# Four weight casts of the first block, each written in two halves one attention unit apart

## The reference, cut to what matters

```python
hx = rms_norm(x, norm_pre[l]) * (1.0 + sc_x) + sh_x
px = hx @ w_in                 # 1024 x 4096
qa, ka, va, ga, bb, cb, ub, gb = jnp.split(px, 8, axis=-1)
s = jnp.einsum('bqhmd,bkhmd->bhmqk', q, k).astype(jnp.float32) * (A_QK ** -0.5)
p = jax.nn.softmax(s, axis=-1)
a = p[:, :, 0] - lam * p[:, :, 1]
o = jnp.einsum('bhqk,bkhd->bqhd', a, v.astype(jnp.float32))
```

## Time and profile before

| | us |
|---|---|
| median of 3 runs | 1646.39 |
| the three runs | 1647.64, 1646.39, 1641.05 |
| the profiled execution | 1641.94 |
| its span | 1640.2 |
| TensorE busy in the span | 1532.1 (93%) |
| ScalarE busy in the span | 665.6 (41%) |

### The profile page before, as it was taken

One profiled execution on the slowest core, in us unless ns is written; L12 is line 12 of the kernel. 1 busy time (PEld: TensorE's weight loads), 2 busy tenths in 40 slices (PEclk: granted clock), 3 DMA queues, 4 the chain that ended last, 5 costly groups with the idle time before them and its releaser, 6 DMA issues. The chain is left out here.

```text
span 1640.2 us, 29691 instructions
## 1 busy us (share of the span) xinstructions
PE 1532.1 (93%) x12509; PEld 1311.9 (80%) x12509; DVE 763.1 (47%) x1244; ACT 665.6 (41%) x1087; POOL 421.7 (26%) x107
## 2 busy tenths in 40 slices
PE   4899999999999999998989999977879999999998
PEld 3688898888887878987879897846768888888786
DVE  3544137777775510137854425468563333433002
ACT  2411216766653411127754444362354444344112
POOL 1422221111140243220022342200034333444342
PEclk9999999999999999999999999989999999999999
DMA  9244462244041032146220532000021222222321
GB/s 376 110 155 155 155 181 65 65 104 104 27 159 47 1 128 83 47 146 162 46 103 3 178 99 91 1 0 3 4 105 52 103 102 102 95 85 77 129 86 68
DMA packets 32598, 155.76 MB, mean 95 GB/s; under 512 B 6744, under 2 KB 8280, under 8 KB 18016
## 3 DMA queue, kind: packets, MB, share of 16 engines
q1 hardware_dynamic: 31168, 153.24, 28.3%
q10 hardware_dynamic: 1312, 0.80, 0.2%
HBM read 132.01 MB, written 2.10 MB: 82 GB/s over the span
## 5 line engine op out<-in xcount | busy, mean ns | idle before, releaser
L215 PE MATMUL banks<-ffn_token_parts,ffu_weight_parts 128*128 128x512 f32 (+1 forms) x1056 | 229.6, 380 | 1.2 <-POOL ffu_weight_parts L196 0.9
L215 PEld LDWEIGHTS banks<-ffn_token_parts,ffu_weight_parts 128*128 128x128 f32 x1056 | 191.7, 188 | 39.0 <-POOL ffu_weight_parts L196 1.1
L196 POOL TENSOR_TENSOR even_weight_parts<-weight_chunk,even_weight_parts 128x2048 fp32r<-128x2048 f32 x16 | 74.6, 4663 | 322.9 <-ACT even_weight_parts L190 322.9
L196 POOL TENSOR_TENSOR ffu_weight_parts<-weight_chunk,ffu_weight_parts 128x2048 fp32r<-128x2048 f32 x22 | 101.6, 4619 | 157.3 <-ACT ffu_weight_parts L190 157.3
L215 PE MATMUL banks<-even_token_parts,even_weight_parts 128*128 128x512 f32 x720 | 133.4, 345 | 0.0
L215 PEld LDWEIGHTS banks<-even_token_parts,even_weight_parts 128*128 128x128 f32 x720 | 110.8, 188 | 20.6 <-issue 3.8
L871 PE MATMUL banks<-even_token_parts,even_weight_parts 128*128 128x512 f32 (+1 forms) x576 | 122.3, 347 | 0.0
L3035 PE MATMUL banks<-ffd_weight_parts,ffn_f_parts 128*128 128x512 f32 x528 | 120.1, 389 | 1.6 <-PEq L2936 1.6
L3035 PEld LDWEIGHTS banks<-ffd_weight_parts,ffn_f_parts 128*128 128x128 f32 x528 | 99.0, 188 | 22.5 <-issue 2.0
L215 PE MATMUL banks<-sec_token_parts,sec_weight_parts 128*128 128x512 f32 (+1 forms) x528 | 114.1, 373 | 0.3 <-PEq L283 0.3
L3013 DVE SCALAR_TENSOR_TENSOR ffn_conv<-banks,b_ffn_taps,ffn_conv 128x511 f32<-128x511 f32 (+1 forms) x88 | 61.8, 744 | 111.9 <-ACT ffn_conv L2985 108.8
(11 more groups left out here) (449 smaller groups left out, 2808.5 us busy)
## 6 DMA issues: line engine op xcount, KB each, us to landing
weight_chunk<-in_ffn_up SPq DMA_DIRECT2D x22, 1024.0 KB, 4.8
weight_chunk<-in_w_in_even SPq DMA_DIRECT2D x16, 1024.0 KB, 6.9
front_late<-in_w_mod SPq DMA_DIRECT2D x16, 1024.0 KB, 4.9
weight_chunk<-in_w_in SPq DMA_DIRECT2D x13, 1024.0 KB, 4.8
weight_chunk<-in_w_out SPq DMA_DIRECT2D x12, 1024.0 KB, 5.4
weight_chunk<-in_w_in_odd SPq DMA_DIRECT2D x12, 1024.0 KB, 4.8
weight_chunk<-in_ffn_down SPq DMA_DIRECT2D x11, 1024.0 KB, 4.9
front_w<-in_w_mod SPq DMA_DIRECT2D x8, 1024.0 KB, 13.3
```

The source lines that it names most:

```text
L196: self.nc.gpsimd.tensor_tensor(parts[:, 1], self.env.raw[s][:], parts[:, 0].bitcast(F32), ALU.subtract).then_inc(self.lo_done, 1)
L215: m = self.nc.tensor.matmul(o, w, env.tok[:, tp, k, a:b], start=n == 0, stop=n == 3 * KD - 1)
```

## The change

The high parts of chunks 12 to 15 are no longer cast by one instruction after unit `c_after(n)`. The first four of the eight rows of k (1024 of 2048 columns a partition) are cast there, the other four after the next unit, `c_after(n) + 1`. Only the second half raises `hi_done`. Both wait for the same semaphores as the whole cast did. The second half stands ahead of the convolution copy (L1032) that follows the same unit for n = 21 and 23.

```diff
+    def hi_half(self, act, i, s, half, freed):
+
+        act.wait_ge(self.env.raw_in[s], self.base[s] + 16 + 16 * i)
+        act.wait_ge(*freed)
+        k = slice(half * KD // 2, (half + 1) * KD // 2)
+        m = self.nc.scalar.copy(self.slot(2 * i + s, s)[:, 0, k], self.env.raw[s][:, k])
+        if half:
+            m.then_inc(self.hi_done, 1)
...
                         if u == c_after(n):
                             if not product(n):
                                 copied(n)
-                            if n % 2 and chunk(n) + 2 < ring.chunks:
+                        for half in range(2):
+                            if u == c_after(n) + half and n % 2 and chunk(n) + 2 < ring.chunks:
                                 c = chunk(n) + 2
-                                ring.hi(act, c // 2, c % 2, (c_ready, n - EARLY + 1))
+                                ring.hi_half(act, c // 2, c % 2, half, (c_ready, n - EARLY + 1))
```

## The result

The changed kernel takes 1660.02 us (median of 6 runs, 1652.7 to 1662.08) against 1644.82 us for the kernel before (6 runs, 1641.05 to 1651.52). The ratio is 1.0074, 95% interval [1.0046, 1.0102]. The forecast was 1644.0 us, with 1638.6 to 1648.5 as range. The profiled execution has a span of 1658.5 us, 18.3 us more than before.

A forecast was written before the change was run, and what follows sets the result against it. TensorE, busy for 93% of the span, was taken as the bound, stalled by ScalarE's casts. Gains of 0.85 + 0.44 + 0.85 + 0.23 = 2.4 us off the median before gave 1644.0 us, range 1638.6 to 1648.5.

The forecast's parts named there:

- The stall and its shrinking: Behind the four casts, TensorE's L760 waits of 1.92, 0.99, 1.51 and 1.74 us for ScalarE's copy each shrink by 0.85 us.
- The second half, unit by unit: One unit after each cast, the second half gives some of 0.85 us back; gains 0.85, 0.44, 0.85 and 0.23 us.
- the third: Third cast's next unit: the second half is hidden because TensorE runs at half clock there; no wait, gain 0.85 us.
- an unfallen clock: Third place with the clock staying at 2.4 GHz: L760 is held by the copy until about 381.72, gain 0.99 us.
- What is moved, and who waits: `hi_done` and GpSimd's low part come 3 to 4 us later; cover of 27 us and more, so nothing is lost.
- Full gain: Rival, 15%: the second half meets more slack; 3.4 us, or 5.1 us with a clock fall avoided, 1641.3 us.
- no gain: Rival, 20%: the second half gives all back; 0.4 us slower to 1.2 us faster, 1645.2 to 1646.8 us.
- Slower: Rival, 5%: shifted, more frequent small waits let TensorE's clock fall elsewhere, up to 1.75 us each; 1649.2 us with three.

The follow-up runs named there:

- the two pairs without holds: Half casts against whole casts, with low parts of 64 columns (0.9966 and 1.0006) and with low parts halved from chunk 11 on (0.994 and 0.9962 of before).
- e2_same_unit: The changed kernel with both half casts back to back behind the same unit, where the whole cast stood; 0.9998 of the kernel before.

## Why the prediction was wrong

The measured 1660.02 us lie 11.5 us above the high end of the range, and the time moved the other way.

**The stall and its shrinking: right.** Forecast were waits behind the first halves of 1.07, 0.14, 0.66 and 0.89 us. They are 1.06, 0.15, 0.65 and 0.90. The half cast takes 1.046 us (forecast 1.05):

```profile
L197 ACT CAST even_weight_parts<-weight_chunk x8: 1036/1046/1058, 300.2 to 435.8; 128x1024 fp32r<-128x1024 f32 x8
```

**The second half, unit by unit: right but for the third.** Forecast were no wait, 0.41, none and 0.62 us one unit later; there are none, 0.49, 1.59 and 0.29. The third, the changed kernel:

```profile
394.92 0.78 ACT L979 COPY da_turned<-banks 128x768 f32<-128x768 f32 x1
...
395.76 0.66 PE L769 MATMUL banks<-even_v,da_turned 128*128 128x64 f32 x4 [1.59 <-ACT da_turned L979]
```

It is the case that the prediction gave for an unfallen clock, in which L760 is held by the copy. By its numbers TensorE then asks for the copy at 382.71 - 0.85 - 1.75 = 380.11 and gets it at 381.72, a wait of 1.61 us, with a gain of 0.99 us against 0.85. So the waits for the copy sum to only 0.5 us less than in the earlier trace rows and not 2.4: TensorE, at full clock, waits for a copy that it reached later at half the clock before.

**"What is moved, and who waits": here it failed.** The sentence was that behind `hi_done` on GpSimd stands only the next chunk's low part, and the low part's move was costed at nothing, with the cover of its consumer. The consumer indeed never waited. What I left out is who can't work while the low part runs. VectorE's combination has two operands in SBUF, and beside the low part, which reads SBUF, it was held for up to 4.57 us. Before, the cast of 1.90 us let the combination of its unit pass, and the low part mostly ended ahead of the next one. VectorE at chunk 12, the kernel before:

```profile
296.36 0.48 DVE L1180 SCALAR_TENSOR_TENSOR da_exp_zero<-da_exp_one,da_ratio,da_exp_zero 128x256 f32<-128x256 f32 x1
...
302.28 0.22 DVE L1178 SCALAR_TENSOR_TENSOR da_ratio<-da_recip,neg_lam,da_sums 128x1 f32<-128x1 f32 x1
```

The low part ran between the two, from 297.40 to 301.96. In the changed kernel the last piece of the cast takes 1.05 us, and the low part started ahead of the combination at chunks 12 and 15 and within 0.04 us of it at chunk 13. Price: 7.0 us of waits, where the forecast gain was 2.4 us and the two pairs without holds show 1.5 us fewer waits for the copy. That the holds cost the time is shown by the short low parts (0.9966), by the writes without reads (0.9977), by the two unequal cuts, and by the halved low parts, which keep the half casts and lose the waits.

The Trainium skill says it in "SBUF — State Buffer", section "Who interferes with whom": a VectorE instruction with two inputs in SBUF contends with a GpSimd instruction that reads SBUF, not with one that only writes, and the later one is blocked until the other ends; one with at most one input there, outside VectorE's two-port modes, does not contend. The runs agree: 4.14 and 5.37 us beside the subtraction, 0.22 and 1.02 us beside the writes, 0.16 us for the reciprocal with its one input. Only at a lead of 0.02 or 0.04 us was the operation held that the profile reports as the earlier one. It was the rule to weigh, and the prediction weighed another.

**The rivals.** Full gain and no gain were both told in waits for ScalarE's copy, and neither held a cost of VectorE. "Slower" was given 5%, by the granted clock. Its mechanism is there in part: 17.2 us at half clock in the profiled execution against 3.5 of before. Two of its three stretches stand at waits for VectorE. But the first lies ahead of all half casts, and `e2_same_unit`, without such a wait behind chunks 12 to 15, had 0.96 over 246 to 475 us as well; its profiled execution took 1655.59 us, its median is 1646.93. So the clock scatters the time of one kernel by several microseconds, and it isn't settled how much of the loss beyond the 7.0 us comes by way of it: the four kernels with the fewest waits had a mean clock of 0.99 or 1.00 here, the changed one 0.96 and 0.97 in its two profiles.

**The range** was built from the costs of ScalarE and some of a fall of the clock, and so could not hold a cost of another pair of engines.

## What to carry to other kernels

Shortening one engine's instruction also moves the instruction that it releases; ask which engines can't run beside that one, not only who waits for its result. An operation whose duration varies in a trace (0.22, 0.92 and 3.60 us for one column) shows such a hold: look at what ended at the same moment. A long GpSimd operation beside a VectorE chain can be cut to pieces that fit between the chain's two-input operations, each released by the end of the last one; here that gave 0.9962, and 0.994 with the half casts.

## What the runs showed of the hardware

The hold is whole and not shared: VectorE's one-column operation ends within 0.02 us of GpSimd's (310.38 and 310.37; 261.69 and 261.68), and the long one of chunk 13, which takes 1.02 us alone, ended 0.81 us behind it (357.87 and 357.06). Which engine is held was decided within less than 0.1 us of reported time. A VectorE operation that is reported 0.02 or 0.04 us ahead of GpSimd's was held for 4.57 and 5.37 us, while one with 0.08 us of lead ran its 1.02 us and GpSimd's operation took 5.38 us instead of 4.53. ScalarE and TensorE were not slowed beside it: in the changed kernel an exponential of 768 columns took 0.90 us beside a low part (306.23) and 0.90 us away from one (344.14), and four matmuls of L880 took 1.17 us in both places (353.68 and 349.74).
